# FFN of a two-layer trunk on one core: a sixth contraction pair by the 2x2 recurrence, and a new order of the groups

## The chip, the cores and the metric

The kernel runs on one NeuronCore of one Trainium2 chip. TensorE (PE) multiplies matrices, VectorE (DVE) and ScalarE (ACT) work on elements, GpSimd (POOL) and SyncE (SP) only issue DMAs in the part looked at here. The metric is the device time of one execution in microseconds; lower is better.

## The reference

The input x is 256 rows of width 2048. Two layers run one after the other, each a mixer (a recurrence with a gating unit in layer 0, windowed attention in layer 1) and a dense SwiGLU channel mixer with D_FF = 5632. The change touches the second alone:

```python
def swiglu(h, w_in, w_out):
    g, u = jnp.split(h @ w_in, 2, axis=-1)
    return (jax.nn.silu(g) * u) @ w_out
# for each layer: x = x + mixer(...); x = x + swiglu(rms_norm(x, ffn_norm), w_ffn_in, w_ffn_out)
```

All inputs are float32. Each product is computed in three matmuls of rounded parts: hi times hi, hi times lo, lo times hi.

## The kernel before, in words

**Blocks.** The hidden width is cut in 11 column blocks of 512 (`FB`). Block 0 runs in an older form ("rounds" of chunks). Blocks 1 to 10 are the block loop (`BLOCKS` = 10 per layer, 20 in all), whose first and last block are written out on each engine and whose others are a hardware loop.

**Groups.** A block has 12 groups of weights, 128 partitions x 4 x 512 each. Groups 0 to 7 (`GROUPS_UP`) are the up projection: each takes a pair of 128-row slices of the contraction (16 slices, 8 pairs), for the gate and the up columns. Groups 8 to 11 are the down projection of the block before, one for each 512 columns of the output. A *plain* up group (`plain_group`, L1754) does 8 products of 3 matmuls, into banks 4 to 7 of PSUM. A *Strassen* group (`strassen_group`, L1766) does the same 2x2 product (two slices x two halves of the rows, against gate and up) in 7 products, 21 matmuls, into banks 0 to 6: P1, P6, P7, P5 are banks 0 to 3, and P2, P4, P3 are banks 4 to 6. It needs three sums of weights (`w_sum`) and four sums of activations (`s_hi`, `s_lo`, made once a layer for `PAIRS` pairs). Before, the order is P S S S P S S P, five Strassen pairs. A down group (`down_group`, L1781) does 24 matmuls into banks 0 and 1 or 2 and 3 in turn (`PAIR[n % 2]`). So P1, P6, P7, P5 and the down groups share banks 0 to 3.

**How a group is prepared.** SP loads it in two DMAs into one of 6 raw buffers (`load_group`, L338). VectorE makes the sums of a Strassen group in three steps (`sum_group`, L1251: L1257 in place, L1261, L1263); the second step waits until the group four earlier is used up. ScalarE casts the raw part to `group_hi` (one of 4 buffers, free when the group four earlier is used), in one instruction for a plain or down group (L717), in two for a Strassen group: L710 after the first step of the sums, L713 after the third. VectorE then subtracts to get the low parts (`lo_group`, L1266: L1275, and L1280 for the sums). TensorE waits for `group_lo_ready` before each group.

**The end of the up groups.** When the last Strassen group is done, ScalarE copies P1 (`copy_p1`, L724), VectorE forms three sums (`out_sums`, L1291) after its low parts of group 9, then those of group 10, then `out_parts` (L1308), which waits for group 7 on TensorE, then those of group 11, then, with ScalarE's silu, the hidden values (`hidden`, L1194), and their 32x32 block transposes (`turn_blocks`, L1204). Each engine works its list strictly in order. So VectorE comes to group 0 of the next block after all of these.

**The output y.** ScalarE copies each down group's result n out of PSUM (`copy_y`, L734) into one of two y buffers (n % 2); POOL adds it to x by an accumulating DMA (`add_y`, L424). A buffer is free again when its DMA has landed, so copy n = 2 waits for the landing of n = 0, and copy 3 for that of 1. TensorE waits for copy 0 before down group 10 and for copy 1 before group 11, since they use the same banks; before P1 of the next block it waits for all four. In POOL's list the DMA of y 0 is followed by `carry_out` (L408, the hidden block to DRAM), y 1, `carry_in` (L418, four DMAs back, as rows), y 2 and y 3.

**ScalarE's order in a block** (L754 on; `before` is the block before):

```python
hi_(0)
if not first:
    copy_y(before, layer, 0)
    copy_y(before, layer, 1)
hi_(1)
if not first:
    copy_y(before, layer, 2)
hi_(2)
if not first:
    copy_y(before, layer, 3)
```

After it come groups 3 and 4, `rows_hi`, groups 5 to 9, `copy_p1`, groups 10 and 11, and silu. In the last block of a layer, the copies of its own y come directly after silu.

The functions that the diff touches follow.

## Time and profile before

| | |
|---|---|
| median of 2 runs | 2021.87 us (2021.65 to 2022.08) |
| profiled execution | 2022.84 us |
| its span, first to last instruction | 2021.0 us |
| TensorE busy | 2009.5 us, 99% of the span |
| VectorE busy | 1650.8 us, 82% |
| ScalarE busy | 1179.5 us, 58% |
| POOL busy | 170.7 us, 8% |
| mean granted TensorE clock | 0.999 |

A busy share is an average over the mixers and the FFN. A matmul's record is longer than the step to the next one, as matmuls are pipelined, so the step is taken from a stretch and a count. "Idle before" names what ended the engine's idle time ahead of an instruction. The issue of a DMA and its landing are two times.

### The profile page before, as it was taken

What the parts mean: (1) busy time and instruction counts of PE and PEld (TensorE: products, weight loads), DVE (VectorE), ACT (ScalarE), POOL (GpSimd) and SP (SyncE); (2) the same over time, 40 slices, a digit from 0 to 9 for tenths busy, and PEclk for the clock granted to TensorE, in tenths of its full rate; (3) what the DMA queues carried; (4) which work ended last, traced back from release to release, by engine and by line L of the source; (5) the groups of instructions that cost most, each with busy time, mean ns of one, the idle gap of its engine ahead of it and who ended that gap; (6) DMA issues with size and microseconds to landing.
All of it is one profiled execution on the core that took longest, in us unless ns stands there. A gap on an engine that the chain in (4) does not pass through costs nothing.

```text
span 2021.0 us, 24668 instructions
## 1 busy us (share of the span) xinstructions
PE 2009.5 (99%) x9269; PEld 1666.7 (82%) x9269; DVE 1650.8 (82%) x1560; ACT 1179.5 (58%) x1195; POOL 170.7 (8%) x216
## 2 busy tenths in 40 slices
PE   9999999999999999999999999999999999999998
PEld 7888888888888888888888887888888888888886
DVE  5666777779999999999986467779999999999995
ACT  6745645555665555656557466555656556655554
POOL 0000000100111110111100000100111101111010
PEclk9999999999999999999999999999999999999999
DMA  8755443856988888888887644767888888888885
GB/s 270 236 189 165 160 145 129 282 195 229 270 257 257 245 241 265 261 259 251 239 241 227 197 140 144 232 221 231 260 259 254 238 254 266 260 253 245 245 262 158
DMA packets 237187, 461.40 MB, mean 228 GB/s; under 512 B 16480, under 2 KB 21376, under 8 KB 236992
## 3 DMA queue, kind: packets, MB, share of 16 engines
q1 hardware_dynamic: 202832, 386.97, 56.9%
q0 software_dynamic: 30496, 69.22, 16.8%
q10 hardware_dynamic: 3792, 4.34, 0.7%
q8 instruction: 39, 0.64, 0.1%
q14 instruction: 28, 0.23, 0.0%
HBM read 401.10 MB, written 17.29 MB: 207 GB/s over the span
## 4 chain that ended last, share of the span: by engine, by line
PE 92%; DVE 5%; ACT 2%; DMA 1%; issue 1%; ACTq 0%; SPq 0%; DVEq 0%
PE ps L1749 58%; PE ps L1534 29%; DVE g_lo L1275 1%; PE ps L1640 1%; DVE w_lo L917 1%; DVE w_lo L1280 1%; DMA raw<-in_w_ab_in 1%; DVE w_sum L1263 0%; PE ps L1900 0%; PE ps L1875 0%; ACT junk L508 0%; PE ps L1560 0%; ACT w_hi L465 0%; PE ps L1566 0%; PE ps L1888 0%
## 5 line engine op out<-in xcount | busy, mean ns | idle before, releaser
L1275 DVE TENSOR_TENSOR g_lo<-g_raw,g_hi 128x2048 fp32r<-128x2048 f32 x240 | 547.3, 2288 | 55.1 <-ACT g_hi L717 32.0
L917 DVE TENSOR_TENSOR w_lo<-raw,w_hi 128x1024 fp32r<-128x1024 f32 x248 | 294.7, 1221 | 145.3 <-ACT w_hi L465 138.7
L717 ACT CAST g_hi<-g_raw 128x2048 fp32r<-128x2048 f32 x140 | 265.5, 1911 | 157.3 <-PE ps L1749 151.4
L465 ACT ACTIVATE w_hi<-raw 128x1024 fp32r<-128x1024 f32 x248 | 254.1, 1056 | 140.2 <-DMA raw<-in_w_ab_in 52.0
L710 ACT CAST g_hi<-g_raw 128x2048 fp32r<-128x2048 f32 x100 | 191.5, 1915 | 215.9 <-DVE g_raw L1257 215.9
L1749 PE MATMUL ps<-g_hi,xT_hi 128*128 128x512 f32 x780 | 303.6, 389 | 0.6 <-DVE w_lo L1280 0.5
L1749 PE MATMUL ps<-g_hi,xT_lo 128*128 128x512 f32 x780 | 303.4, 389 | 0.0
L1534 PE MATMUL ps<-w_hi,xT_hi 128*128 128x512 f32 x672 | 264.5, 394 | 0.6 <-DVE w_lo L917 0.5
L1749 PE MATMUL ps<-g_lo,xT_hi 128*128 128x512 f32 x680 | 264.5, 389 | 0.0
L1534 PE MATMUL ps<-w_hi,xT_lo 128*128 128x512 f32 x672 | 261.8, 390 | 0.0
L1534 PE MATMUL ps<-w_lo,xT_hi 128*128 128x512 f32 x672 | 261.5, 389 | 0.0
L1749 PE MATMUL ps<-g_hi,h0T_hi 128*128 128x512 f32 x640 | 249.1, 389 | 0.0
L1749 PE MATMUL ps<-g_hi,h0T_lo 128*128 128x512 f32 x640 | 249.0, 389 | 0.0
L1749 PE MATMUL ps<-g_lo,h0T_hi 128*128 128x512 f32 x640 | 249.0, 389 | 0.0
L424 POOL DMA_DIRECT2D x<-y x80 | 95.9, 1199 | 984.4 <-ACT y L734 699.9
L1280 DVE TENSOR_TENSOR w_lo<-w_sum,g_hi 128x1536 fp32r<-128x1536 f32 x100 | 175.1, 1751 | 0.0
L1749 PEld LDWEIGHTS ps<-g_hi,xT_hi 128*128 128x128 f32 x780 | 146.4, 188 | 31.7 <-DVE w_lo L1280 1.4
L1749 PEld LDWEIGHTS ps<-g_hi,xT_lo 128*128 128x128 f32 x780 | 146.4, 188 | 30.4
L1749 PE MATMUL ps<-g_hi,s_hi 128*128 128x512 f32 x400 | 155.6, 389 | 0.0
L1749 PE MATMUL ps<-g_hi,s_lo 128*128 128x512 f32 x400 | 155.6, 389 | 0.0
L713 ACT CAST g_hi<-w_sum 128x1536 fp32r<-128x1536 f32 x100 | 148.5, 1485 | 10.1 <-DVE w_sum L1263 8.8
L1749 PEld LDWEIGHTS ps<-g_lo,xT_hi 128*128 128x128 f32 x680 | 127.6, 188 | 26.4
(225 smaller groups left out, 3047.5 us busy)
## 6 DMA issues: line engine op xcount, KB each, us to landing
g_raw<-in_w_ffn_in SPq DMA_DIRECT2D x320, 512.0 KB, 4.9
g_raw<-in_w_ffn_out SPq DMA_DIRECT2D x160, 512.0 KB, 4.8
raw<-in_w_ab_in SPq DMA_DIRECT2D x96, 512.0 KB, 4.7
x<-y POOLq DMA_DIRECT2D x80, 512.0 KB, 6.9
raw<-in_w_qkv SPq DMA_DIRECT2D x40, 512.0 KB, 4.6
raw<-in_w_ab_out SPq DMA_DIRECT2D x32, 512.0 KB, 5.3
raw<-in_w_ffn_in SPq DMA_DIRECT2D x32, 512.0 KB, 4.6
raw<-in_w_c_out SPq DMA_DIRECT2D x32, 512.0 KB, 4.7
```

Of the source, the lines that this page charges most:

```text
L424: pool.dma_start(x[:, :, n * W:(n + 1) * W], y[n % 2][:, :, :], accum_op=ALU.add).then_inc(y_landed[n % 2], 16)
L465: act.activation(w_hi[:, s, :], raw[:, s % RAWS, :], ACT.Copy).then_inc(hi_ready, 1)
L710: act.copy(dst[:, 0:4, :].rearrange("p s w -> p (s w)"), src[:, :, :].rearrange("p s w -> p (s w)")).then_inc(group_hi_ready, 1)
L713: act.copy(dst[:, 4:7, :].rearrange("p s w -> p (s w)"), w_sum[g % 4][:, :, :].rearrange("p s w -> p (s w)")).then_inc(group_hi_ready, 1)
L717: act.copy(dst[:, 0:4, :].rearrange("p s w -> p (s w)"), src[:, :, :].rearrange("p s w -> p (s w)")).then_inc(group_hi_ready, 1)
L917: dve.tensor_tensor(w_lo[:, s, :], raw[:, s % RAWS, :], w_hi[:, s, :], ALU.subtract).then_inc(lo_ready, 1)
L1275: ins = dve.tensor_tensor(lo_part[:, 0:4, :].rearrange("p s w -> p (s w)"), src[:, :, :].rearrange("p s w -> p (s w)"), hi_part[:, 0:4, :] ...
L1280: ins = dve.tensor_tensor(sum_lo[g % 4][:, :, :].rearrange("p s w -> p (s w)"), w_sum[g % 4][:, :, :].rearrange("p s w -> p (s w)"), hi_pa ...
L1534: ins = pe.matmul(banks[:, t, :], a[:, k0 + h, ts], w[:, s, h * W:(h + 1) * W], start=first and h == 0 and i == 0, stop=last and h == 1 an ...
L1640: ins = pe.matmul(side[t][:, c], E[:, t, c], E[:, t, c], start=True, stop=True)
L1749: ins = pe.matmul(bank, a, w, start=first and i == 0, stop=last and i == 2)
```

## The change

The plain pair 5 becomes a Strassen pair. The order of the up groups is now S S S P S S S P. Group g uses hi and sum buffer `HI_OF[g % 4]`, so that the buffer without room for 7 slots goes to the plain and down groups; s_lo moves in part over constants that the FFN does not read. Each Strassen group does P2, P4, P3 (banks 4 to 6) first, then P1, P6, P7, P5. TensorE's wait for the four y copies moves from the start of group 1 to just before P1 of group 0, and ScalarE's copy 3 moves between the two casts of group 2.

```diff
--- before.py
+++ after.py
@@ -75,8 +75,9 @@
 
 
 BLOCKS = FB - 1
-GROUPS_UP = [("plain", 5), ("strassen", 0), ("strassen", 1), ("strassen", 2),
-             ("plain", 6), ("strassen", 3), ("strassen", 4), ("plain", 7)]
+GROUPS_UP = [("strassen", 0), ("strassen", 1), ("strassen", 2), ("plain", 6),
+             ("strassen", 3), ("strassen", 4), ("strassen", 5), ("plain", 7)]
+HI_OF = [3, 1, 2, 0]
 N_UP = len(GROUPS_UP)
 BLOCK_GROUPS = N_UP + GROUPS
 LAST_STRASSEN = max(g for g, (kind, _) in enumerate(GROUPS_UP) if kind == "strassen")
@@ -136,6 +137,7 @@
         scratch = bias_at + 8 * KB
         place[0] = scratch + 76 * KB
         u_mid = sb("u_mid", [P, W])
+        consts_at = place[0]
         consts = sb("consts", [P, N_CONST, P])
         junk = sb("junk", [P, W])
         cols = sb("cols", [P, 80])
@@ -194,7 +196,8 @@
         sum_lo = [None] + [sb(f"w{i}_lo", [P, 3, W], F32R, at=bias_at + (16 + 6 * i) * KB) for i in range(1, 4)]
         s_size = 512 * PAIRS
         s_hi = [sb(f"s{i}_hi", [P, PAIRS, P], F32R, at=bias_at + 40 * KB + i * s_size) for i in range(4)]
-        s_lo = [sb(f"s{i}_lo", [P, PAIRS, P], F32R, at=bias_at + 50 * KB + i * s_size) for i in range(4)]
+        s_lo_at = [bias_at + 52 * KB, bias_at + 55 * KB, consts_at + 512, consts_at + 512 + s_size]
+        s_lo = [sb(f"s{i}_lo", [P, PAIRS, P], F32R, at=s_lo_at[i]) for i in range(4)]
         s_sum = sb("s_sum", [P, 4, PAIRS, P], at=bias_at + 60 * KB)
         x_sum = sb("x_sum", [P, PAIRS, 2, T], at=bias_at + 22 * KB)
         gu = sb("gu", [P, 4, W], at=bias_at + 68 * KB)
@@ -696,22 +699,24 @@
             def free_group(f, layer, g, first, base):
 
                 if first and g < 4:
-                    act.wait_ge(chunk_used, RING * base + (0, 12, 15, 0)[g])
+                    act.wait_ge(chunk_used, RING * base + (0, 12, 15, 0)[HI_OF[g]])
                 else:
                     act.wait_ge(group_used, f * BLOCK_GROUPS + (group_at(layer, 0) + g - 3))
 
-            def hi_group(f, layer, g, first, base):
+            def hi_group(f, layer, g, first, base, between=None):
 
                 free_group(f, layer, g, first, base)
-                src, dst = group_raw[g % 6], group_hi[g % 4]
+                src, dst = group_raw[g % 6], group_hi[HI_OF[g % 4]]
                 if g < N_UP and GROUPS_UP[g][0] == "strassen":
                     n = 3 * (STRASSEN_BEFORE[g] - PAIRS)
                     act.wait_ge(sum_step, f * (3 * PAIRS) + (layer * BLOCKS * 3 * PAIRS + n + 1))
                     act.copy(dst[:, 0:4, :].rearrange("p s w -> p (s w)"),
                              src[:, :, :].rearrange("p s w -> p (s w)")).then_inc(group_hi_ready, 1)
+                    if between is not None:
+                        between()
                     act.wait_ge(sum_step, f * (3 * PAIRS) + (layer * BLOCKS * 3 * PAIRS + n + 3))
                     act.copy(dst[:, 4:7, :].rearrange("p s w -> p (s w)"),
-                             w_sum[g % 4][:, :, :].rearrange("p s w -> p (s w)")).then_inc(group_hi_ready, 1)
+                             w_sum[HI_OF[g % 4]][:, :, :].rearrange("p s w -> p (s w)")).then_inc(group_hi_ready, 1)
                 else:
                     act.wait_ge(pair_landed[g % 6], f * 64 + (32 * (group_at(layer, 0) // 6 + g // 6 + 1)))
                     act.copy(dst[:, 0:4, :].rearrange("p s w -> p (s w)"),
@@ -758,9 +763,7 @@
                     hi_(1)
                     if not first:
                         copy_y(before, layer, 2)
-                    hi_(2)
-                    if not first:
-                        copy_y(before, layer, 3)
+                    hi_group(f, layer, 2, first, base, None if first else lambda: copy_y(before, layer, 3))
                     hi_(3)
                     hi_(4)
                     if not first:
@@ -1250,7 +1253,7 @@
 
             def sum_group(f, layer, g, first):
 
-                b, w = group_raw[g % 6], w_sum[g % 4]
+                b, w = group_raw[g % 6], w_sum[HI_OF[g % 4]]
                 n = 3 * (STRASSEN_BEFORE[g] - PAIRS)
                 step = f * (3 * PAIRS) + (layer * BLOCKS * 3 * PAIRS + n)
                 dve.wait_ge(pair_landed[g % 6], f * 64 + (32 * (group_at(layer, 0) // 6 + g // 6 + 1)))
@@ -1265,7 +1268,7 @@
 
             def lo_group(f, layer, g):
 
-                src, hi_part, lo_part = group_raw[g % 6], group_hi[g % 4], group_lo[g % 6]
+                src, hi_part, lo_part = group_raw[g % 6], group_hi[HI_OF[g % 4]], group_lo[g % 6]
                 strassen = g < N_UP and GROUPS_UP[g][0] == "strassen"
                 ready = f * HI_DONE[-1] + ((layer * BLOCKS - 1) * HI_DONE[-1] + HI_DONE[g])
                 dve.wait_ge(group_hi_ready, ready - 1 if strassen else ready)
@@ -1277,8 +1280,8 @@
                                         hi_part[:, 0:4, :].rearrange("p s w -> p (s w)"), ALU.subtract)
                 if strassen:
                     dve.wait_ge(group_hi_ready, ready)
-                    ins = dve.tensor_tensor(sum_lo[g % 4][:, :, :].rearrange("p s w -> p (s w)"),
-                                            w_sum[g % 4][:, :, :].rearrange("p s w -> p (s w)"),
+                    ins = dve.tensor_tensor(sum_lo[HI_OF[g % 4]][:, :, :].rearrange("p s w -> p (s w)"),
+                                            w_sum[HI_OF[g % 4]][:, :, :].rearrange("p s w -> p (s w)"),
                                             hi_part[:, 4:7, :].rearrange("p s w -> p (s w)"), ALU.subtract)
                 ins.then_inc(group_lo_ready, 1)
 
@@ -1753,34 +1756,36 @@
 
             def plain_group(g, first, last):
 
-                hi_part, lo_part = group_hi[g % 4], group_lo[g % 6]
+                hi_part, lo_part = group_hi[HI_OF[g % 4]], group_lo[g % 6]
                 for q in range(4):
                     k = 2 * GROUPS_UP[g][1] + q // 2
                     for t in range(NT):
                         ts = slice(t * P, (t + 1) * P)
                         bank = ((P2, P4), (P3, C22))[q % 2][t]
                         ins = product(bank, xT_hi[:, k, ts], xT_lo[:, k, ts], hi_part[:, q, :], lo_part[:, q, :],
-                                      first and q < 2, last and q >= 2)
+                                      first and q == 1 and t == 1, last and q >= 2)
                 ins.then_inc(group_used, 1)
 
-            def strassen_group(g, first, last):
-
-                hi_part, lo_part, sums_lo = group_hi[g % 4], group_lo[g % 6], sum_lo[g % 4]
+            def strassen_group(g, first, last, shared_free):
+
+                hi_part, lo_part, sums_lo = group_hi[HI_OF[g % 4]], group_lo[g % 6], sum_lo[HI_OF[g % 4]]
                 p = GROUPS_UP[g][1]
                 t0, t1 = slice(0, P), slice(P, T)
                 x_part = lambda k, ts: (xT_hi[:, k, ts], xT_lo[:, k, ts])
                 s_part = lambda i: (s_hi[i][:, p, :], s_lo[i][:, p, :])
-                for bank, a, slot, alone in ((P1, x_part(2 * p, t0), 0, True), (P6, s_part(1), 4, True),
-                                             (P7, s_part(2), 5, True), (P5, s_part(0), 1, True),
-                                             (P2, x_part(2 * p + 1, t0), 2, False), (P4, x_part(2 * p + 1, t1), 6, False),
-                                             (P3, s_part(3), 3, False)):
+                for bank, a, slot, alone in ((P2, x_part(2 * p + 1, t0), 2, False), (P4, x_part(2 * p + 1, t1), 6, False),
+                                             (P3, s_part(3), 3, False),
+                                             (P1, x_part(2 * p, t0), 0, True), (P6, s_part(1), 4, True),
+                                             (P7, s_part(2), 5, True), (P5, s_part(0), 1, True)):
+                    if slot == 0:
+                        shared_free()
                     w_lo_part = lo_part[:, slot, :] if slot < 4 else sums_lo[:, slot - 4, :]
-                    ins = product(bank, *a, hi_part[:, slot, :], w_lo_part, alone and first, alone and last)
+                    ins = product(bank, *a, hi_part[:, slot, :], w_lo_part, first, alone and last)
                 ins.then_inc(group_used, 1)
 
             def down_group(g):
 
-                hi_part, lo_part = group_hi[g % 4], group_lo[g % 6]
+                hi_part, lo_part = group_hi[HI_OF[g % 4]], group_lo[g % 6]
                 n = g - N_UP
                 for k in range(4):
                     for t in range(NT):
@@ -1796,15 +1801,19 @@
                 chunks(base + 1, 0, 8, *X, PAIR[1])
 
                 def block(f, first, last):
+
+                    def shared_free():
+                        if first:
+                            pe.wait_ge(silu_ready, 2 * FB * layer + 2)
+                            pe.wait_ge(hid_ready, 2 * FB * layer + 2)
+                        else:
+                            pe.wait_ge(y_copied, f * 4 + 4 * (layer * BLOCKS - 1))
+
                     for g in range(BLOCK_GROUPS):
+                        if g == 0 and first:
+                            pe.wait_ge(s_ready, 4 * (layer + 1))
                         if g == 0 and not first:
                             pe.wait_ge(out_step, f * 5 + 5 * (layer * BLOCKS - 1))
-                        if g == 1 and first:
-                            pe.wait_ge(silu_ready, 2 * FB * layer + 2)
-                            pe.wait_ge(hid_ready, 2 * FB * layer + 2)
-                            pe.wait_ge(s_ready, 4 * (layer + 1))
-                        if g == 1 and not first:
-                            pe.wait_ge(y_copied, f * 4 + 4 * (layer * BLOCKS - 1))
                         if g == N_UP:
                             pe.wait_ge(hT_ready, f * 2 + 2 * FB * layer)
                             pe.wait_ge(out_step, f * 5 + (5 * (layer * BLOCKS - 1) + 1))
@@ -1818,9 +1827,9 @@
                         if g >= N_UP:
                             down_group(g)
                         elif GROUPS_UP[g][0] == "strassen":
-                            strassen_group(g, g == 1, g == LAST_STRASSEN)
+                            strassen_group(g, g == 0, g == LAST_STRASSEN, shared_free if g == 0 else lambda: None)
                         else:
-                            plain_group(g, g == 0, g == N_UP - 1)
+                            plain_group(g, g == 3, g == N_UP - 1)
 
                 block(1, True, False)
                 with pe.Fori(2, FB - 1) as f:
```

## Rows read from the trace of the kernel before

**Rows 1.** The page, part 1: busy time, share of the span and instructions of each engine
```profile
PE 2009.5 (99%) x9269; PEld 1666.7 (82%) x9269; DVE 1650.8 (82%) x1560; ACT 1179.5 (58%) x1195; POOL 170.7 (8%) x216
```
**Rows 2.** Waits of TensorE, whole span: us in total, times, longest us
```profile
PE ps L1749 <- DVE w_lo L1280: 0.5, 1, 0.5
```
**Rows 3.** One lap as a window: us, busy (instructions), clock, DMA share, GB/s
```profile
core 0: us, PE busy (x) PEld busy (x) DVE busy (x) ACT busy (x) POOL busy (x), PEclk, DMA share, GB/s
742.32:804.19 61.87, 61.87 (x275) 51.23 (x274) 56.72 (x42) 36.49 (x26) 7.67 (x9) 1.00 0.85 254
```
**Rows 4.** Timeline of VectorE, one Strassen group: start us, us, operation, [idle before]
```profile
704.73 0.69 DVE L1257 TENSOR_TENSOR g_raw<-g_raw 128x512 f32<-128x512 f32 x1
...
707.52 2.29 DVE L1275 TENSOR_TENSOR g_lo<-g_raw,g_hi 128x2048 fp32r<-128x2048 f32 x1
709.73 1.75 DVE L1280 TENSOR_TENSOR w_lo<-w_sum,g_hi 128x1536 fp32r<-128x1536 f32 x1
711.40 2.29 DVE L1275 TENSOR_TENSOR g_lo<-g_raw,g_hi 128x2048 fp32r<-128x2048 f32 x1
```
**Rows 5.** Timeline of VectorE, end of one block and start of the next
```profile
733.98 2.29 DVE L1275 TENSOR_TENSOR g_lo<-g_raw,g_hi 128x2048 fp32r<-128x2048 f32 x1 [1.33 <-ACT g_hi L717]
737.41 0.69 DVE L1295 TENSOR_TENSOR u_mid<-ps,gu 128x512 f32<-128x512 f32 x1 [1.14 <-ACT gu L724]
...
742.32 2.36 DVE L1308 TENSOR_TENSOR gu<-ps,gu 128x1024 f32<-128x1024 f32 x2
...
748.33 1.30 DVE L1204 STREAM_TRANSPOSE hid_blk<-hid 128x512 f32<-128x512 f32 x2
749.69 2.29 DVE L1275 TENSOR_TENSOR g_lo<-g_raw,g_hi 128x2048 fp32r<-128x2048 f32 x1
...
753.11 0.69 DVE L1261 TENSOR_TENSOR w_sum<-g_raw 128x512 f32<-128x512 f32 x1 [0.52 <-PE ps L1749]
...
756.06 2.29 DVE L1275 TENSOR_TENSOR g_lo<-g_raw,g_hi 128x2048 fp32r<-128x2048 f32 x1 [1.00 <-ACT g_hi L710]
```
**Rows 6.** Timeline of ScalarE over the four y copies
```profile
747.75 1.92 ACT L717 CAST g_hi<-g_raw 128x2048 fp32r<-128x2048 f32 x1 [2.37 <-PE ps L1749]
749.56 1.01 ACT L734 COPY y<-ps 128x1024 f32<-128x1024 f32 x1
753.11 1.02 ACT L734 COPY y<-ps 128x1024 f32<-128x1024 f32 x1 [2.54 <-PE ps L1749]
...
758.55 1.02 ACT L734 COPY y<-ps 128x1024 f32<-128x1024 f32 x1 [1.24 <-PE ps L1749]
...
764.53 1.02 ACT L734 COPY y<-ps 128x1024 f32<-128x1024 f32 x1 [0.32 <-DMA x<-y]
```
**Rows 7.** Timeline of POOL: the DMAs of y 0 and y 1
```profile
750.94 1.18 POOL L424 DMA_DIRECT2D x<-y  x1 [33.59 <-ACT y L734]
751.65 1.06 POOL L408 DMA_DIRECT2D hid_dram<-hid_blk  x1
756.08 1.18 POOL L424 DMA_DIRECT2D x<-y  x1 [3.37 <-issue]
```
**Rows 8.** L424, windows on the y 1 issues at 756.1, 1796 and 570.4
```profile
DMA to landing us min/median/max: 8.4/8.4/8.4
...
DMA to landing us min/median/max: 7.5/7.5/7.5
...
DMA to landing us min/median/max: 9.8/9.8/9.8
```
**Rows 9.** Waits of the y copies, whole span: us in total, times, longest
```profile
ACT y L734 <- DMA x<-y: 4.0, 6, 1.8
```
**Rows 10.** Timeline of the first block of layer 0: three engines
```profile
440.40 1.91 ACT L717 CAST g_hi<-g_raw 128x2048 fp32r<-128x2048 f32 x1 [2.90 <-DMA g_raw<-in_w_ffn_in]
...
454.03 0.39 PE L1749 MATMUL ps<-g_hi,xT_hi 128*128 128x512 f32 x1
...
495.43 2.35 DVE L1308 TENSOR_TENSOR gu<-ps,gu 128x1024 f32<-128x1024 f32 x2
```
**Rows 11.** Timeline of TensorE at the kernel's start
```profile
1.46 6.70 PE L1566 MATMUL ps<-warm 128*128 128x512 f32 x17 [1.46 <-DVE warm L987]
```

## Prediction

> **What bounds the kernel now.** I read the profile from the busy shares to single laps. By its busy time TensorE works 99% of the span and no other engine is near that [rows 1], and the waits of TensorE hold one entry of 0.5 us in all the FFN blocks [rows 2]. So a matmul taken away there shortens the kernel, unless something else closes in behind. One lap of the block loop, from one `out_parts` (L1308) to the next, takes 61.87 us with TensorE busy all of it [rows 3]. The code issues 3 plain groups of 24 matmuls, 5 Strassen groups of 21 and 4 down groups of 24 in a lap, 273 in all: 61.87 / 273 = 0.2266 us each (the window counts 275, since those at its edges overlap).
>
> VectorE is the next. A Strassen group costs it 6.67 us from first start to the following group's start (704.73 to 711.40), made of sums 2.79 (to 707.52), the low part 2.21 and the sums' low part 1.67 [rows 4]. A plain group costs only the 2.2. VectorE's waits in a lap are 1.33, 1.14, 0.52 and 1.00 us [rows 5], 4.0 in all; the other 57.9 are work, with nothing between. That is all the cover there is for more VectorE work.
>
> **The change part by part.** I take t = 0 at the start of `out_parts` in the profiled lap, 742.32 [rows 5].
>
> *Matmuls.* A plain group becomes a Strassen group: 3 matmuls fewer, 270 x 0.2266 = 61.2 us a lap, a gain of 0.68 us. Over 20 laps (10 blocks, 2 layers) that is 13.6 us at best.
>
> *VectorE.* One Strassen group more instead of a plain one: +6.67 - 2.2 = +4.47 us. 57.9 + 4.5 = 62.4 us a lap, more than before's 61.87 even with no wait left. ScalarE gets 1.5 us more casts, VectorE's few `s_sum` and `s_lo` operations before the block loop grow by a fifth of their width; the first lies in ScalarE's 25 us of idle time a lap, the second in the wait for the first weights. The loads are the same 12 a lap. The permutation `HI_OF` costs nothing: before, a hi buffer already came back after four groups, and still does. The moved constants cost nothing, as nothing reads the masks in the FFN.
>
> *Group 0 is now Strassen.* This is what decides. ScalarE's order is: cast group 0 of the next block, then copy y 0, then y 1. A plain group 0 was cast as soon as its buffer was free (747.75, t = 5.4), copy 0 ended at 750.57 (t = 8.25), and TensorE wanted it for down group 10 at t = 10.8, when down group 9 ends [rows 6]. Now the second half of that cast waits for VectorE's sums of group 0, and these stand behind `out_parts`, group 11, `hidden` and `turn_blocks`: VectorE is free for them at 749.69, t = 7.37 [rows 5]. Plus sums 2.79 gives 10.16, plus the cast of the sums 1.40 and the copy 1.01: copy 0 ends at t = 12.6, 4.3 later. Down group 10 waits 1.8 us (12.6 - 10.8), then groups 10 and 11 end at 18.0 and 23.5.
>
> *POOL and the shared banks.* Copy 3 of y needs y buffer 1 back, that is the accumulating DMA of y 1. POOL issued y 0 0.37 us after copy 0 ended, y 1 5.14 us after that [rows 7], and it landed 8.4 us later in this lap; the narrowest and widest I found are 7.5 and 9.8 [rows 8]. `carry_out` lies between the two issues and moves with them. I take 8.0, as most laps lie under this one. Landing: 12.6 + 0.37 + 5.14 + 8.0 = 26.1; copy 3 ends at 27.1. Before, this landing fell together with the end of group 11 (t = 21.6): copy 3 waited for it 6 times in 80 copies, at most 1.8 us [rows 9], and TensorE still had the whole plain group 0, 5.4 us, before it touched the banks. Now only 9 matmuls stand before P1: 23.5 + 2.04 = 25.5. So P1 waits until 27.15, 1.6 us. This bit of cover was lost with the plain group 0; the reordering of banks gives back 2.04 of 5.44.
>
> *Closing the lap.* TensorE: from P1 there are 12 matmuls of group 0 and 153 of groups 1 to 7, 165 x 0.2266 = 37.4: t = 64.6. VectorE: the cast of group 2's sums now stands behind copy 3, so it ends at 27.1 + 1.40 = 28.5, and VectorE waits some 3 us for it. From there 1.67 for that low part, 2.2 (group 3), 6.67 (4), 1.14 (`rows_lo`), 13.3 (5, 6), 6.6 (7 to 9), 2.6 (`out_sums`), 2.2 (10): t = 64.9. The later one sets the lap: with 0.1 of latency 65.0 us, 3.1 more than before. This runs in the 9 laps between the blocks of a layer: 18 x 3.1 = +56 us. In the last block of a layer the copies follow at once.
>
> *The first block of a layer.* Its group 0 was cast at 440.40, when its data came, and TensorE reached it at 454.03 [rows 10]. VectorE now does 6.67 + 6.67 + 2.7 from 440.40 before `hidden`, which ends at 457.9; TensorE has 2.04 us of work there and waits 1.8. Going on, group 6 is ready at 486.3 and `out_parts` begins at 497.6 instead of 495.43 [rows 10]: +2.2 us, twice, +4.4.
>
> Sum: 2022.8 us, the profiled execution's own, + 56 + 4.4 = 2083. The median shown is 1.0 under that execution, so **2082 us**.
>
> **The rivals.**
> 1. *The y 1 transfer lands in time* (by t = 24.4; 1.7 sooner than I take). For it: without a `carry_out` behind y 0 nothing says what y 1 costs, and weight loads, which share the engines, thin out while TensorE waits. Against it: 7.5 is the least I saw, and that gives 25.6. Then only the wait for copy 0 stays: 12.6 + 10.9 + 2.04 + 37.4 = 62.9, lap 63.0, 18 x 1.1 + 4.4 = +24: 2046 us. The Trainium skill (DMA: Bandwidth & Descriptors, Anatomy of one DMA) fits a DMA issued from GpSimd as a fixed part of 2.0 us plus bytes over 436 GB/s; for 512 KB that is an estimate of 3.2 us, by which this rival would be the forecast. The rows do not agree (8.4, never under 7.5 in the loop for y 1), so I keep the rows.
> 2. *The gain shows* (the other side: not slower). It needs copy 0 to end before t = 10.8, 1.8 us sooner than worked out, and VectorE's 62.4 to shrink by over 1 us. For it: TensorE is the bound in every row. Against it: VectorE is in order, and t = 7.37 is read, not guessed. Price: -13.6 us, 2008 us.
> 3. *The transfer gets later still*, as at its 9.8, each lap: +1.8 x 18 = 32: 2114 us. Once in 20 laps so far.
> 4. *The new waits lower TensorE's clock.* The granted clock is at full level (2.4 GHz) in the loop, a matmul each 0.2266 us; the first 17 of the kernel, after idleness, took 6.70 us, 0.39 each [rows 11]. If one such stretch followed in each of the 18 laps, 17 x 0.17 = 2.8 us each, +51: 2133 us. Against it: the waits are 1.8 and 1.6 us, with 10.9 us of dense matmuls between. The Trainium skill (TensorE: Matmul & The Clock Gate, Part 1) says that the array falls back to half rate after a stretch of idleness; no row shows a wait of this length in the loop, so neither does one show the fall.
>
> **How the numbers follow.** Forecast 0.66, with its own range 2064 to 2100 (y 1 landing after 7.5 to 9); rival 1 0.18; rival 2 0.04; rival 3 0.08; rival 4 0.04. The range of 2045 to 2100 leaves out rivals 2 to 4 and a little of the tails. Two per cent, about what a measurement of this kernel can tell from no change, lies at 2062 us: slower is the forecast without its lowest edge and rivals 3 and 4, 0.75; within 2% is rival 1, rival 2 and that edge, 0.24; faster by 2% would need 40 us where the matmuls hold 13.6: 0.01.
>
> **What would show it.** In the profile after: 60 matmuls fewer; a lap near 65.0 us; TensorE with two waits a lap, before down group 10 on the y copy (1.8 us) and within group 0 on the y copy (1.6 us); the first y copy at t = 11.6 instead of 7.2; the last waiting for the accumulating DMA in every lap; VectorE waiting about 3 us for the cast of the sums in group 2, and no more for the copy of P1. It would be wrong if laps come out at 63.0 (rival 1), at 61.2 (rival 2), or if the granted clock falls.

## The result, and the profile after

The changed kernel takes **2118.75 us** (2118.52 to 2118.98) against 2021.87 before: ratio 1.0476, 95% interval 1.046 to 1.0493. Slower, as forecast, but 37 us beyond the forecast and 19 beyond the range.

The lines of the changed kernel stand 3 to 5 further down: `out_parts` is L1311, the y copy L739, its DMA L427, the matmuls L1752, the casts L713 and L718 (Strassen) and L722, the first sum step L1260, the sums' low part L1283.

The page, part 1, of the kernel after, which answers to [rows 1]:

```profile
PE 2026.2 (96%) x9209; PEld 1666.6 (79%) x9209; DVE 1738.5 (82%) x1640; ACT 1209.3 (57%) x1215; POOL 170.4 (8%) x216
```

The waits of TensorE in it (us in total, times, longest), against [rows 2]:

```profile
PE ps L1752 <- ACT y L739: 73.1, 36, 3.2
PE ps L1752 <- DVE hid L1197: 6.4, 2, 3.7
```

The 60 matmuls are gone (9269 to 9209), yet TensorE is busy 17 us longer, and it waits 36 times for a y copy, twice in each of 18 laps. Two laps as windows, against [rows 3], and a stretch inside the second (same columns):

```profile
766.20:832.10 65.90, 61.95 (x272) 50.68 (x271) 60.76 (x47) 38.02 (x27) 7.66 (x9) 1.00 0.80 239
832.10:900.40 68.30, 63.24 (x271) 51.55 (x271) 61.05 (x47) 37.78 (x27) 7.63 (x9) 0.98 0.79 230
861.10:864.50 3.40, 3.40 (x8) 2.71 (x9) 2.10 (x2) 3.03 (x2) 0.22 (x1) 0.50 0.49 182
```

There are two kinds of laps: 8 of 18 take 65.1 to 66.1 us (mean 65.80), 10 take 67.1 to 68.3 (mean 67.49). In the second kind the granted clock falls to 0.5, the lower of the two levels (1.2 GHz). The timeline of TensorE there, just after its wait before P1:

```profile
861.01 0.78 PE L1752 MATMUL ps<-g_hi,xT_hi 128*128 128x512 f32 x1 [3.17 <-ACT y L739]
861.60 0.63 PE L1752 MATMUL ps<-g_lo,xT_hi 128*128 128x512 f32 x1
862.02 0.63 PE L1752 MATMUL ps<-g_hi,xT_lo 128*128 128x512 f32 x1
...
864.78 0.40 PE L1752 MATMUL ps<-g_hi,s_hi 128*128 128x512 f32 x1
865.01 0.39 PE L1752 MATMUL ps<-g_lo,s_hi 128*128 128x512 f32 x1
```

The step from start to start is 0.42 to 0.43 us (861.60 to 862.02) and then 0.23 again (864.78 to 865.01): some seven or eight matmuls at 0.2 us extra, 1.4 to 1.6 us a fall.

The lap from 766.24 on, ScalarE's timeline, against [rows 6]:

```profile
774.15 1.92 ACT L713 CAST g_hi<-g_raw 128x2048 fp32r<-128x2048 f32 x1 [4.86 <-DVE g_raw L1260]
776.24 1.48 ACT L718 CAST g_hi<-w_sum 128x1536 fp32r<-128x1536 f32 x1 [0.17 <-DVE w_sum L1266]
777.62 1.92 ACT L739 COPY y<-ps 128x1024 f32<-128x1024 f32 x2
...
784.59 1.02 ACT L739 COPY y<-ps 128x1024 f32<-128x1024 f32 x1 [0.19 <-PE ps L1752]
...
793.08 1.01 ACT L739 COPY y<-ps 128x1024 f32<-128x1024 f32 x1 [3.66 <-DMA x<-y]
793.99 1.48 ACT L718 CAST g_hi<-w_sum 128x1536 fp32r<-128x1536 f32 x1
```

Copy 0 starts at t = 11.38, behind the two casts, which wait for VectorE. Copy 3 waits 3.66 us for a DMA, and the last cast stands behind it. POOL's timeline and the two landings (windows on the issues), against [rows 7, 8]:

```profile
778.99 1.18 POOL L427 DMA_DIRECT2D x<-y  x1 [41.48 <-ACT y L739]
779.71 1.06 POOL L411 DMA_DIRECT2D hid_dram<-hid_blk  x1
784.82 1.18 POOL L427 DMA_DIRECT2D x<-y  x1 [4.06 <-issue]
```

```profile
DMA to landing us min/median/max: 5.5/5.5/5.5
...
DMA to landing us min/median/max: 8.2/8.2/8.2
```

And VectorE, which waits for that last cast:

```profile
773.47 0.65 DVE L1260 TENSOR_TENSOR g_raw<-g_raw 128x512 f32<-128x512 f32 x1
...
795.50 1.76 DVE L1283 TENSOR_TENSOR w_lo<-w_sum,g_hi 128x1536 fp32r<-128x1536 f32 x1 [3.63 <-ACT g_hi L718]
```

TensorE's wait before down group 10 in that lap, the first of its two:

```profile
778.75 0.49 PE L1752 MATMUL ps<-g_hi,h0T_hi 128*128 128x512 f32 x1 [1.76 <-ACT y L739]
```

So the forecast's mechanism is all there: copy 0 late, the wait before down group 10, the late landing of y 1, the wait before P1. What was not in it is y 0's landing at 5.5 instead of 4.8, and the clock. y 0's landing matters because POOL's issue of y 1 follows it by 0.34 to 0.36 us in all laps, before and after. The difference in spans is 95.7 us: 18 laps take 1201.2 us instead of 1112.4 (+88.8), and the first blocks take 2.2 and 4.6 us more.

### The profile page after: what moved, and what is told of

The parts are those of the page before. It is cut to its first block, busy times and chain, and to the rows that moved or that the text cites. A ratio compares the mean times of both kernels' runs of the same rounds, so it can differ in the third digit from the quotient of the medians.

```text
span 2116.7 us, 24468 instructions
## 1 busy us (share of the span) xinstructions
PE 2026.2 (96%) x9209; PEld 1666.6 (79%) x9209; DVE 1738.5 (82%) x1640; ACT 1209.3 (57%) x1215; POOL 170.4 (8%) x216
## 4 chain that ended last, share of the span: by engine, by line
PE 56%; DVE 20%; issue 10%; DMA 8%; ACT 4%; POOL 2%; ACTq 0%; DVEq 0%; SPq 0%; POOLq 0%
PE ps L1537 26%; PE ps L1752 26%; DMA x<-y 7%; DVE g_lo L1278 6%; DVE w_sum L1266 2%; DVE w_lo L1283 2%; DVE gu L1311 1%; ACT y L739 1%; DVE w_sum L1264 1%; DVE g_raw L1260 1%; DVE hid L1197 1%; PE ps L1643 1%; POOL x L427 1%; DVE w_lo L920 1%; DVE gu L1300 1%
## 5 line engine op out<-in xcount | busy, mean ns | idle before, releaser
L713 ACT CAST g_hi<-g_raw 128x2048 fp32r<-128x2048 f32 x120 | 229.8, 1915 | 357.7 <-DVE g_raw L1260 357.7
L1752 PE MATMUL ps<-g_hi,xT_hi 128*128 128x512 f32 x680 | 268.1, 394 | 47.3 <-ACT y L739 40.9
L1752 PE MATMUL ps<-g_hi,h0T_hi 128*128 128x512 f32 x640 | 251.1, 392 | 32.2 <-ACT y L739 32.2
L722 ACT CAST g_hi<-g_raw 128x2048 fp32r<-128x2048 f32 x120 | 226.4, 1910 | 75.7 <-PE ps L1752 75.7
L1752 PE MATMUL ps<-g_hi,xT_lo 128*128 128x512 f32 x680 | 265.5, 390 | 0.0
L1283 DVE TENSOR_TENSOR w_lo<-w_sum,g_hi 128x1536 fp32r<-128x1536 f32 x120 | 210.2, 1752 | 66.7 <-ACT g_hi L718 66.7
L1752 PE MATMUL ps<-g_hi,h0T_lo 128*128 128x512 f32 x640 | 249.2, 389 | 0.0
L1752 PE MATMUL ps<-g_lo,h0T_hi 128*128 128x512 f32 x640 | 249.1, 389 | 0.0
L1752 PE MATMUL ps<-g_lo,xT_hi 128*128 128x512 f32 x560 | 218.9, 391 | 0.0
L1752 PE MATMUL ps<-g_hi,s_lo 128*128 128x512 f32 x480 | 193.9, 404 | 0.0
L1752 PE MATMUL ps<-g_hi,s_hi 128*128 128x512 f32 x480 | 193.6, 403 | 0.0
L1752 PEld LDWEIGHTS ps<-g_hi,xT_hi 128*128 128x128 f32 x680 | 129.0, 190 | 82.0 <-ACT y L739 48.5
L718 ACT CAST g_hi<-w_sum 128x1536 fp32r<-128x1536 f32 x120 | 178.0, 1483 | 12.7 <-DVE w_sum L1266 11.2
L427 POOL DMA_DIRECT2D x<-y x80 | 95.9, 1198 | 1078.1 <-ACT y L739 794.1
L1752 PEld LDWEIGHTS ps<-g_hi,h0T_hi 128*128 128x128 f32 x640 | 120.1, 188 | 64.0 <-issue 35.5
L1266 DVE TENSOR_TENSOR w_sum<-g_raw,w_sum 128x1024 f32<-128x1024 f32 x120 | 147.0, 1225 | 4.1
```

What stands on the lines that cost most here:

```text
L427: pool.dma_start(x[:, :, n * W:(n + 1) * W], y[n % 2][:, :, :], accum_op=ALU.add).then_inc(y_landed[n % 2], 16)
L713: act.copy(dst[:, 0:4, :].rearrange("p s w -> p (s w)"), src[:, :, :].rearrange("p s w -> p (s w)")).then_inc(group_hi_ready, 1)
L718: act.copy(dst[:, 4:7, :].rearrange("p s w -> p (s w)"), w_sum[HI_OF[g % 4]][:, :, :].rearrange("p s w -> p (s w)")).then_inc(group_hi_rea ...
L722: act.copy(dst[:, 0:4, :].rearrange("p s w -> p (s w)"), src[:, :, :].rearrange("p s w -> p (s w)")).then_inc(group_hi_ready, 1)
L1266: dve.tensor_tensor(w[:, 1:3, :], b[:, 0:4:2, :], w[:, 0:1, :].broadcast_to([P, 2, W]), ALU.subtract).then_inc(sum_step, 1)
L1283: ins = dve.tensor_tensor(sum_lo[HI_OF[g % 4]][:, :, :].rearrange("p s w -> p (s w)"), w_sum[HI_OF[g % 4]][:, :, :].rearrange("p s w -> p ...
```

## The experiments

In all experiments t counts from the start of `out_parts`, and the ratios are to the kernel before on the same chip.

### Order or volume?

**order_five_pairs**: back to five Strassen pairs, in the new order.

```diff
-GROUPS_UP = [("strassen", 0), ("strassen", 1), ("strassen", 2), ("plain", 6),
-             ("strassen", 3), ("strassen", 4), ("strassen", 5), ("plain", 7)]
+GROUPS_UP = [("strassen", 0), ("strassen", 1), ("strassen", 2), ("plain", 5),
+             ("strassen", 3), ("strassen", 4), ("plain", 6), ("plain", 7)]
```

> The changed kernel with five Strassen pairs again (the order is S S S P S S P P; matmuls and VectorE work as in the kernel before), all else as changed. Queue theory (copy 0 of y stands behind the cast of a Strassen group 0, which stands behind VectorE's end-of-block work): the waits of TensorE before down group 10 (1.9 us) and before P1 (2.4 us) stay; a clean lap is 27.95 + 168 x 0.2266 + 0.1 = 66.1 us, and clock falls add about 0.8 a lap on average: 2105 to 2125 us. Volume theory (the sixth pair's 4.5 us of VectorE work a lap costs the time): laps of 61.9 us again, 2020 to 2030 us.

Measured: 2135.83 us, ratio 1.0552 (1.0534 to 1.0569). An undisturbed lap as a window:

```profile
702.10:768.29 66.19, 62.44 (x275) 51.08 (x274) 56.87 (x43) 36.50 (x26) 7.65 (x9) 1.00 0.80 238
```

66.19 against 66.1 expected, with VectorE's work of before. It is even slower than the changed kernel, and above my range, as its clock fell in 16 of the 18 laps, not in 10. The volume theory falls: the order alone costs more than the whole loss.

**copy0_first**: one line moved in ScalarE's list.

```diff
-                    hi_(0)
                     if not first:
                         copy_y(before, layer, 0)
+                    hi_(0)
+                    if not first:
                         copy_y(before, layer, 1)
```

> The changed kernel with ScalarE's copy of y 0 moved ahead of the cast of group 0. Queue theory: copy 0 starts at t = 5.4 instead of 11.4, both waits of TensorE go, no clock fall in the loop, the lap is set by VectorE's work alone at 62.2 to 62.5 us: 2022 + 18 x 0.5 + 7 for the first blocks = 2038 (2032 to 2046) us. Volume theory: the wait before down group 10 goes, the lap hardly changes, as VectorE was full anyway: over 2090 us. A theory in which the landing of y 1 is a matter of load on the DMA engines and not of its issue: only the 1.9 us before group 10 goes, 2118 - 18 x 1.9 = 2084 us.

Measured: **2034.75 us**, ratio 1.0058 (1.0042 to 1.0075). 84 of the 97 us are gone. A lap of it, and the wait that TensorE still has for copies:

```profile
747.70:809.83 62.13, 61.50 (x271) 50.60 (x270) 60.69 (x47) 37.79 (x27) 7.67 (x9) 1.00 0.84 253
```

```profile
PE ps L1753 <- ACT y L739: 11.3, 18, 0.9
```

No wait before down group 10, one of at most 0.9 us before P1, and no fall of the clock in any lap. VectorE is busy 60.69 of 62.13 us, and its longest pause in the lap is 0.13 us; the lap is its own.

**plain_first_six**: six Strassen pairs, group 0 plain, buffers as before.

```diff
-GROUPS_UP = [("strassen", 0), ("strassen", 1), ("strassen", 2), ("plain", 6),
-             ("strassen", 3), ("strassen", 4), ("strassen", 5), ("plain", 7)]
-HI_OF = [3, 1, 2, 0]
+GROUPS_UP = [("plain", 6), ("strassen", 0), ("strassen", 1), ("strassen", 2),
+             ("plain", 7), ("strassen", 3), ("strassen", 4), ("strassen", 5)]
+HI_OF = [0, 1, 2, 3]
```

(The start and end flags of the accumulations, and the wait before P1, move with it.)

> Six Strassen pairs, but in the order P S S S P S S S with buffers as before, so that group 0 is plain and cast early. Queue theory: no wait of TensorE for a y copy; the lap is set by VectorE's 62.4 us of work and by down group 8 waiting for the sum of P1 now that the last up group is Strassen: 62.5 to 63.2 us a lap, 2022 + 18 x 1.0 + 2 = 2042 (2032 to 2050) us. Volume theory: as slow as the changed kernel, over 2090 us. If VectorE's volume cost nothing: 2008 us.

Measured: 2081.27 us, ratio 1.0294 (1.0277 to 1.0311). Between the theories, and no forecast held. A lap, and VectorE's waits in laps 2 to 9:

```profile
763.40:827.50 64.10, 61.82 (x272) 50.56 (x271) 60.83 (x48) 37.84 (x26) 7.67 (x9) 1.00 0.83 245
```

```profile
DVE u_mid L1298 <- ACT gu L729: 10.9, 8, 1.4
DVE w_lo L1283 <- ACT g_hi L718: 7.0, 8, 1.6
```

No wait for the cast of group 0, but two new ones on a VectorE that is already full: 1.4 us for the copy of P1, as the last up group is now Strassen, and 0.9 on average for the cast behind copy 3, which I had left between the casts. 62.4 + 1.4 + 0.9 = 64.7; the laps take 63.7 to 67.0. I had let the first wait hide under VectorE's work. With VectorE full nothing hides there. TensorE stands still twice in each of these laps (three times in the first lap of a layer), for 0.4 to 1.7 us at a time, and its clock never falls.

### Why does y 1 land late?

**y1_before_carry**: POOL issues y 1 ahead of the hidden block.

```diff
                     add_y(f - 1, layer, 0)
+                    add_y(f - 1, layer, 1)
                     if f < FB - 1:
                         carry_out(f, layer)
-                    add_y(f - 1, layer, 1)
```

> The changed kernel with POOL's list as y 0, y 1, carry_out instead of y 0, carry_out, y 1. If y 1 lands late because carry_out's small packets are ahead of it in the same queue, it lands about 5.5 us after its issue as in the last blocks (5.4 and 5.6), at t = 24.2, and TensorE's wait before P1 falls from 2.4 to near 0, the clock falls go with it, while the 1.9 us before group 10 stay: lap 63.0 to 63.4, 2022 + 18 x 1.4 + 7 = 2054 (2046 to 2064) us. If the 8 us come from the weight loads that share the engines, nothing changes: 2110 to 2120 us.

Measured: 2111.05 us, ratio 1.0439 (1.0422 to 1.0457). In the lap from 762.4, y 1's issue and landing:

```profile
781.15 1.18 POOL L427 DMA_DIRECT2D x<-y  x1 [4.82 <-issue]
```

```profile
DMA to landing us min/median/max: 7.7/7.7/7.7
```

Issued at nearly the same t (18.8 against 18.6), before `carry_out`, it still takes 7.7 us. Over the 18 laps y 1 takes 7.8 us on average, against 8.0 in the changed kernel. So the packets of `carry_out` could account for some 0.3 us, not for the 2.5 us between 5.5 and 8.

**late_group3_load**: the weights of groups 3 and 4 wait until down group 11 is done.

```diff
-                        sp.wait_ge(group_used, f * BLOCK_GROUPS + (group_at(layer, 0) + g - 5))
+                        sp.wait_ge(group_used, f * BLOCK_GROUPS + (group_at(layer, 0) + g - (3 if g == 3 else 5)))
```

> The changed kernel with the weights of group 3 (and behind them those of group 4) loaded from t = 23.5 on, when down group 11 is done, instead of from t = 10.7 and 18. If the y DMAs take 5.6 and 8.2 us because weight loads share the DMA engines, y 0 lands in 4.8 us and y 1 in 5.4 to 6, at t = 23.5 to 24; copy 3 starts with the end of group 11, the wait before P1 goes; the weights of groups 3 and 4 then land at about t = 29 to 31 and may hold VectorE by 1 or 2 us: 2055 to 2090 us. If y 1 is slow by itself (an accumulating DMA behind another one): it lands at t = 26.8 as in the changed kernel, 2118 us or more.

Measured: 2140.34 us, ratio 1.0577 (1.056 to 1.0595). The landings of y 0 and y 1 in the lap from 771.6:

```profile
DMA to landing us min/median/max: 4.8/4.8/4.8
...
DMA to landing us min/median/max: 5.5/5.5/5.5
```

That part holds: with no weights under way, y 0 takes 4.8 us (in 17 of 18 laps) and y 1 5.1 to 5.7 us. In 17 of 18 laps y 1 lands by t = 23.8, and the wait before P1 is gone. The total is 50 us beyond my range all the same: the weights come late, and TensorE waits for VectorE instead, in all

```profile
PE ps L1752 <- DVE w_lo L1283: 45.7, 34, 1.7
```

and the clock still falls in 12 of the 18 laps, now behind the wait before down group 10, which is 2.2 to 2.4 us here. The late loads cost more than the transfer gave.

### What does the clock cost?

In the three `fill` kernels TensorE does unneeded matmuls into the free bank 7 ahead of its waits.

```diff
+            def fill(n):
+                for _ in range(n):
+                    pe.matmul(C22, xT_hi[:, 0, 0:P], xT_hi[:, 0:2, :].rearrange("p k t -> p (k t)"), start=True, stop=True)
...
+                        if g == N_UP + 2 and not last:
+                            pe.wait_ge(out_step, f * 5 + (5 * (layer * BLOCKS - 1) + 5))
+                            fill(7)
...
                         else:
+                            fill(9)
                             pe.wait_ge(y_copied, f * 4 + 4 * (layer * BLOCKS - 1))
```

**fill_both_waits** (both additions), **fill_first_wait** (`fill(7)` alone), **fill_second_wait** (`fill(9)` alone):

> The changed kernel, and TensorE does 7 unneeded matmuls (1.6 us) into the free bank 7 ahead of its wait before down group 10, and 9 (2.0 us) ahead of its wait before P1, in the 9 laps of a layer that have the waits. The sum is not touched. Clock theory (10 laps of the changed kernel are 1.5 to 1.7 us longer because TensorE's granted clock falls to its lower level after the waits): all laps come out at 65.8 us, no fall of the clock in the loop, 2118 - 17 = 2101 (2097 to 2106) us. If the falls have another cause, or the long laps come from the DMAs: 2114 to 2122 us. If the waits were not idle at all, the matmuls are added: 2118 + 18 x 3.6 = 2183 us.

> As before it, with the 7 matmuls ahead of down group 10 alone; 2.4 us idle stay before P1. If the wait before P1 by itself lets the clock fall (all falls came right after it): 2112 to 2120 us, as the changed kernel. If it takes both waits of a lap: 2101 us.

> As before it, with the 9 matmuls ahead of P1 alone; 1.9 us idle stay before down group 10. If the wait before P1 is what lets the clock fall: 2101 us, laps of 65.8. If the first wait takes part: some laps stay at 67.3, between 2101 and 2118 us.

| kernel | us | ratio (interval) | clock falls within laps |
|---|---|---|---|
| changed kernel | 2118.75 | 1.0476 (1.046 to 1.0493) | 10 |
| fill_first_wait | 2118.64 | 1.0478 (1.046 to 1.0495) | 9 |
| fill_second_wait | 2111.93 | 1.0439 (1.0422 to 1.0457) | 7 |
| fill_both_waits | 2106.11 | 1.0416 (1.0399 to 1.0433) | 0 |

A lap with both filled, busier by 16 matmuls and only 0.2 us longer than the mean of the changed kernel's short laps:

```profile
762.20:828.18 65.98, 65.47 (x287) 53.54 (x287) 60.79 (x47) 37.93 (x27) 7.67 (x9) 1.00 0.80 238
```

Doing 288 more matmuls makes the kernel 12 us faster (1.0476 - 1.0416 = 0.0060 of 2022). That is what the clock costs in all, under the 17 I expected. Two things make the difference: not all of the long laps' 17 us was the clock (see below), and a few laps of fill_both_waits are long for another reason, a y 1 landing of 8.8 to 9.5 us (copy 3 starts 0.08 us later on average than in the changed kernel, 1.5 us over 18 laps). Either wait alone, mostly 2.0 to 2.5 or 1.8 to 2.0 us, is enough for falls (after the P1 wait in the one kernel, after the other wait in the other), which I had not expected of the first. The waits of 0.6 to 0.9 us in copy0_first and of 0.4 to 1.7 us in plain_first_six brought none.

fill_second_wait also tells about y 1 once more. In its 7 laps with a fall down group 10 ends later, and the next weights start later. Two of its laps, one with a fall and one without, in the 5.4 us from y 1's issue on (the queue of the weight loads: packets, MB, share of the 16 engines), and y 1's landing:

```profile
q1 hardware_dynamic: 12, 0.02, 1.2%
x<-y POOLq DMA_DIRECT2D x1, 512.0 KB, 5.9
...
q1 hardware_dynamic: 544, 1.05, 71.0%
x<-y POOLq DMA_DIRECT2D x1, 512.0 KB, 8.1
```

In all 7 such laps y 1 takes 5.4 to 6.1 us, and in the 11 others 7.7 to 9.7. Part of what a fall costs in this kernel comes back in this way, as the wait before P1 goes.

**fill_and_copy3_late**: the same, with copy 3 behind both casts of group 2.

```diff
-                    hi_group(f, layer, 2, first, base, None if first else lambda: copy_y(before, layer, 3))
+                    hi_(2)
+                    if not first:
+                        copy_y(before, layer, 3)
```

> As fill_both_waits (2106 us, laps of 65.9), with copy 3 of y back behind both casts of group 2. Two paths close the lap of the changed kernel: TensorE's (P1 at t = 27.95, then 165 matmuls: 65.4) and VectorE's (the cast of group 2's sums behind copy 3 ends at 29.3, then VectorE's work: 65.8). If both are as told, the lap falls to TensorE's 65.4 and VectorE no longer waits for that cast: 2106 - 18 x 0.4 = 2099 us. If VectorE's path does not set the lap: 2106 us; if the whole wait of 3.7 us of VectorE counted: 2106 - 18 x 3 = 2052 us.

Measured: 2105.38 us, ratio 1.0407 (1.0391 to 1.0423), not to be told from fill_both_waits. From the start of copy 3 to the lap's end it is 38.90 us here (790.39 in the lap 763.5 to 829.3) and 39.05 there: TensorE's path closes the lap only 0.15 us sooner than VectorE's, not 0.4. VectorE's wait of 3.6 us for the cast costs next to nothing, because TensorE stood still for the same DMA.

### A version that beats both

**copy0_hidden_early**: copy0_first, and in a layer's first block VectorE does the hidden values ahead of group 2's sums.

```diff
-                sum_group(1, layer, 2, True)
                 hidden(0, layer, base)
                 turn_blocks(0, layer)
+                sum_group(1, layer, 2, True)
```

> copy0_first (2035 us), and in the first block of a layer VectorE does the hidden values of block 0 and their transposes before the sums of group 2. If the 12 us that copy0_first is over the kernel before are 18 laps x 0.33 us of VectorE's work and 6 us of the two first blocks (TensorE waits 2.6 and 3.7 us there for the hidden values, and its clock falls once or twice behind it), then these waits go and the time is 2022.4 + 6 + (0 to 1) = 2028 (2025 to 2031) us. If the first blocks are bound by VectorE's sums anyway: 2033 to 2036 us.

Measured: 2037.22 us, ratio 1.007 (1.0057 to 1.0084): no gain. The wait for the hidden values shrinks from 7.5 us (two waits) to 2.0, and 5.9 us of waits for low parts come in its place. The other expectation had the cause right, with a range 1 us too low: in the first block VectorE works without a break from the landing of the first weights, 441.5, on, and is late at group 6 anyway.

**sums_started_early**: that, and the first sum step of a Strassen group goes ahead of the work that stood before it: the low part of the group before, `rows_lo` for group 5, the transposes for group 0.

```diff
+            def sum_first(f, layer, g):
+                b = group_raw[g % 6]
+                dve.wait_ge(pair_landed[g % 6], f * 64 + (32 * (group_at(layer, 0) // 6 + g // 6 + 1)))
+                dve.tensor_tensor(b[:, 1, :], b[:, 1, :], b[:, 0, :], ALU.subtract).then_inc(sum_step, 1)
...
                     sum_group(f, layer, g, first)
+                if g in (0, 1, 5):
+                    sum_first(f, layer, g + 1)
+                if g == 3:
+                    sum_first(f, layer, 4)
                 lo_group(f, layer, g)
+                if g == 4:
+                    sum_first(f, layer, 5)
...
                     if not last:
+                        sum_first(f + 1, layer, 0)
                         turn_blocks(f, layer)
```

> copy0_hidden_early, and VectorE does the first of the three sum steps of a Strassen group (L1257 of before) ahead of the low part of the group before it, so that the second step need not wait 0.12 us for the first one's semaphore, and ScalarE's cast starts sooner. If the lap of 62.13 us is VectorE's work and these small waits (six of 0.12, five of 0.06, one of 0.13 us, 1.1 in all), VectorE's lap falls to 61.1 and TensorE's 270 matmuls set it: 61.3 to 61.5 us, with copy 3 earlier and the wait of 0.8 us before P1 gone: 2022.4 - 18 x 0.4 - 1 = 2014 (2010 to 2019) us, faster than both kernels. If the lap is bound by anything else: as copy0_hidden_early.

Measured: **2019.16 us**, ratio 0.9986 (0.9977 to 0.9995) over 11 runs: faster than both kernels, and 0.14% under the one before. A lap of it, and VectorE's waits in four of them:

```profile
743.80:805.00 61.20, 61.20 (x272) 50.71 (x271) 59.89 (x47) 37.67 (x27) 7.68 (x9) 1.00 0.88 257
```

```profile
DVE u_mid L1309 <- ACT gu L729: 2.8, 4, 0.8
```

61.20 = 270 x 0.2267: TensorE never stops in a lap, and VectorE has 0.7 us to spare. What the reordering did on VectorE, a first sum step and the instruction after it, in copy0_first and here:

```profile
777.25 0.69 DVE L1261 TENSOR_TENSOR g_raw<-g_raw 128x512 f32<-128x512 f32 x1
778.06 0.69 DVE L1265 TENSOR_TENSOR w_sum<-g_raw 128x512 f32<-128x512 f32 x1
...
769.87 0.68 DVE L1259 TENSOR_TENSOR g_raw<-g_raw 128x512 f32<-128x512 f32 x1
770.47 2.28 DVE L1283 TENSOR_TENSOR g_lo<-g_raw,g_hi 128x2048 fp32r<-128x2048 f32 x1
```

From start to start it is 0.81 us when the second sum step, which reads what the first wrote, comes next, and 0.60 when another instruction stands between. The laps hold what the change promised, 0.64 us each or 11.5 us in all; the two first blocks take 8 of them back (two kinds of waits for VectorE, 4.3 and 4.4 us in total, and one fall of the clock).

## Why the prediction was right and wrong, point by point

- **Matmuls**: right. 270 in a lap; the 0.68 us show in full once nothing else stands in the way.
- **VectorE's work**: 62.4 us a lap forecast, 62.13 measured in copy0_first. Right as a volume. But about 1.6 us of it were small losses between dependent steps: in sums_started_early 61.20 - 0.7 = 60.5 are left. I had called them work.
- **Copy 0 behind the cast of group 0**: right. t = 12.4 for its end (12.6 forecast), the wait before down group 10 is 1.9 us over the normal step (1.8 forecast). Moving that one copy took away 84 us.
- **The landings**: the mechanism was right, one term was mis-sized. The 5.14 us from y 0's issue to y 1's hold y 0's landing, which I kept at 4.8 us. In the laps it was 5.3 to 6.9, mostly 5.5 to 5.7, since in its new place more of the weights of group 3 travel with it (0.9 MB instead of 0.45 while it is under way); y 1 took 6.0 to 9.1, mostly 8.0 to 8.2, as forecast. Copy 3 mostly starts at 26.8 to 26.9 instead of 26.1, so the short laps are 65.80 instead of 65.0: 18 x 0.8 = 14 us. Of the two things that the y DMAs could be sharing with, `carry_out` and the weight loads, the runs leave the weights.
- **Closing the lap**: from copy 3's start to the end 38.9 us forecast, 39.05 measured.
- **The clock**: the step that failed, a term that the sum put at nothing. The forecast gave it a chance of 0.04 (rival 4) and argued that waits of 1.8 and 1.6 us with dense work between are harmless. They were 1.9 and 2.4 us, and the clock fell in 10 of 18 laps. Rival 4's price of 2.8 us a fall was too high (1.4 to 1.6), its chance far too low. The ten long laps average 1.7 us more than the short ones, 17 us in all. Eight of them are 1.5 us over; the other two, where y 1 took 8.8 and 9.1 us, are longer by another 0.7 and 1.0. So some 15 us are the clock by the rows; the fills show 12 us by cause, and 1.5 more if the later copy 3 in them is counted. The Trainium skill (TensorE: Matmul & The Clock Gate, Part 1) says that idleness lets the array fall back to half rate; the stretch at 0.5 agrees in kind. The argument fails by its own term: the wait before down group 10 came out as forecast, and fill_second_wait, where it is the one that stays, still has 7 falls. Laps whose idle stretches were all 1.7 us or shorter (plain_first_six, fill_both_waits, copy0_first) had none. Which laps fall, and why they almost alternate, stays open.
- **First blocks**: 2.2 us each forecast; 2.2 and 4.6 measured, the second with a longer wait (3.7 us) and a longer slow stretch behind it.
- The parts: 14 us from the landings, 15 from the clock, 2 from the two late landings of y 1, 2.5 from the first blocks; 1.6 more because the 18 laps of before average 61.80 and not 61.87, and by rounding, and 1.2 from taking the median. That is the miss of 37. The range ended at 2100. By these parts the time would be an estimated 2104 us without the falls of the clock, and 2105 with the landings as forecast. So either of the two alone took it out of the range, by little.
- **The forecast's own range**: its lower edge, 2064, does not follow from y 1 landing after 7.5 us; 18 x 0.5 = 9 us under 2082 is 2073. Nothing hangs on it, as the time came out above.
- **Rival 1** (y 1 in time, by a page's figure): the Trainium skill (DMA: Bandwidth & Descriptors, Anatomy of one DMA) gives an estimate of 3.2 us for 512 KB. Even with no weights under way it was 4.8 and 5.5 us here; the measurement decides.

## What to carry to other kernels

Before an operation changes its kind, look at what stands behind it in the same engine's list: here a cast that had waited only for its buffer came to wait for a busy engine, and a copy that the matmuls needed stood behind it. Price a transfer at the place where it will run, not where it ran. And a wait of about 2 us on TensorE is not only its own length: its clock can fall after it, so a bound from gapless laps is too low once the laps have gaps.

## What the runs showed of the hardware

- An accumulating DMA of 512 KB (y 0) landed in 4.8 us with no weight load under way (late_group3_load, 17 of 18 laps), and in 5.3 to 5.9 us beside 0.9 MB of weights (changed kernel, 16 of 18 laps). The second of two (y 1) took 5.1 to 5.7 us without weights, and 7.6 to 9.1 beside 1.0 to 1.2 MB (16 of 18 laps). The bytes alone do not settle it: y 0 took 4.8 us beside 0.45 MB in the kernel before, and 5.7 beside 0.40 MB in plain_first_six.
- One longer idle stretch of TensorE, of 1.8 to 2.0 us in each lap of about 66 us, or one of mostly 2.0 to 2.5 us, let the granted clock fall to 0.5 in 7 or 9 of 18 laps (fill_second_wait, fill_first_wait). Stretches of 0.6 to 0.9 us (copy0_first), or of 0.4 to 1.7 us two or three times a lap (plain_first_six), did so in none. Each fall cost 1.4 to 1.6 us.
- A 128x512 VectorE sum step took 0.60 us to the start of the next instruction when that one did not depend on it. With the dependent step next it was 0.81 us in the looped blocks and 0.72 us in the blocks that are written out, which do the same; where the 0.09 us between the two come from is open. With six such pairs in a lap, a few more like them, and casts that could start sooner, this decided the sign: 1.0070 with them, 0.9986 without.
